# Transpose instructions for turned operands, grouped gathering of modulation units, and two modulation loads asked for later in a two-block transformer kernel

## What is computed

```
for l in (0, 1):                                   # first block, 2 layers of 3 sublayers
    mod = silu(c) @ ada_w[l] + ada_b[l]            # shift, scale, gate for each sublayer, for context and latent
    h = rms_norm(x) * g * (1 + scale) + shift      # before every sublayer
    x = x + 0.5 * gate * swiglu(h)                 # sublayers k = 0, 2, 3, 5
    x = x + gate * gated_delta(h)                  # sublayer k = 1 (two directions, chunks, 8 heads of 128)
    x = x + gate * window_attention(h)             # sublayer k = 4
for l in (0, 1):                                   # second block, latent tokens only
    x = layer_norm(a * x + mixer(x)); x = layer_norm(a * x + conv_ffn(x))
# gated_delta, per chunk: gc = cumsum(g); decay = exp(gc[i] - gc[j]) for i >= j;
# a triangular solve with (beta k k^T) * decay, a state carried between chunks, rms_norm per head
```

## Time and profile before

| | |
|---|---|
| median of 3 runs | 3239.9 us (3236.26 to 3246.45) |
| the profiled execution | 3243.84 us, its span 3241.9 us |
| TensorE busy | 3051.2 us, 94% |
| ScalarE, VectorE, GpSimd busy | 35%, 41%, 48% |
| mean granted TensorE clock | 0.968 of 2.4 GHz |
| DMA | 389.91 MB, mean 120 GB/s |

### The profile page before, as it was taken

The page is one execution under the profiler, slowest core; times in us unless marked ns, Lnnn a source line. Parts: engine busy times, 40 slices in busy tenths (PEclk is TensorE's granted clock), DMA queues, the critical chain, the costliest instruction groups (busy, mean ns, idle before and its releaser), DMA issues.

```text
span 3241.9 us, 54462 instructions
## 1 busy us (share of the span) xinstructions
PE 3051.2 (94%) x22484; PEld 2659.8 (82%) x22484; DVE 1341.2 (41%) x2506; ACT 1149.5 (35%) x1769; POOL 1564.1 (48%) x1207
## 2 busy tenths in 40 slices
PE   5999999999998999998999979889999999999998
PEld 4787778889887787776778876889987998987998
DVE  3222246755554321233212356333455551445551
ACT  2212223323422322213222235333444664444563
POOL 1444444322123344443445530687853688654686
PEclk8999999999998999998999989999999999999999
DMA  7434332210002334434332320344441444441443
GB/s 288 168 124 169 121 108 91 86 45 3 2 3 78 130 123 169 151 115 155 119 135 87 115 80 14 117 176 154 178 156 66 142 169 169 147 153 66 143 171 127
DMA packets 58915, 389.91 MB, mean 120 GB/s; under 512 B 6480, under 2 KB 7760, under 8 KB 21360
## 3 DMA queue, kind: packets, MB, share of 16 engines
q1 hardware_dynamic: 49472, 322.07, 27.7%
q10 hardware_dynamic: 9072, 64.12, 5.5%
q0 software_dynamic: 192, 1.18, 0.1%
HBM read 386.29 MB, written 1.05 MB: 119 GB/s over the span
## 4 chain that ended last, share of the span: by engine, by line
PE 62%; POOL 18%; issue 13%; DVE 3%; ACT 2%; DMA 0%; POOLq 0%; ACTq 0%; DVEq 0%
POOL ring_lo L2619 18%; PE bank L647 16%; PE bank L648 15%; PE bank L649 15%; PE bank L682 2%; PE bank L1244 1%; PE bank L1149 1%; PE bank L1255 1%; PE bank L971 1%; PE bank L936 1%; PE bank L709 1%; PE bank L1137 1%; PE bank L828 1%; DVE core L2519 0%; PE bank L983 0%
## 5 line engine op out<-in xcount | busy, mean ns | idle before, releaser
L2619 POOL TENSOR_TENSOR ring_lo<-ring,w_hi 128x512 fp32r<-128x512 f32 (+1 forms) x832 | 1094.8, 1347 | 1246.5 <-ACT w_hi L1401 1246.1
L649 PE MATMUL bank<-h_hi,ring_lo 128*128 128x256 f32 (+1 forms) x3384 | 1117.6, 330 | 0.0
L647 PE MATMUL bank<-h_hi,w_hi 128*128 128x512 f32 (+1 forms) x2448 | 863.5, 353 | 51.7 <-POOL ring_lo L2619 28.6
L648 PE MATMUL bank<-h_lo,w_hi 128*128 128x512 f32 (+1 forms) x2448 | 849.1, 347 | 0.0
L649 PEld LDWEIGHTS bank<-h_hi,ring_lo 128*128 128x128 f32 x3384 | 652.5, 193 | 59.5 <-issue 0.5
L647 PEld LDWEIGHTS bank<-h_hi,w_hi 128*128 128x128 f32 x2448 | 469.4, 192 | 131.0 <-issue 50.1
L1401 ACT ACTIVATE w_hi<-ring 128x2048 fp32r<-128x2048 f32 (+2 forms) x226 | 395.2, 1749 | 413.3 <-PE bank L649 328.3
L648 PEld LDWEIGHTS bank<-h_lo,w_hi 128*128 128x128 f32 x2448 | 469.9, 192 | 52.8
L649 PE MATMUL bank<-hid_r,ring_lo 128*128 128x256 f32 (+1 forms) x1088 | 364.3, 335 | 0.0
L2025 DVE SCALAR_TENSOR_TENSOR core<-core,bank 128x512 f32<-128x512 f32 (+1 forms) x88 | 54.7, 621 | 651.8 <-ACT core L1469 651.8
L647 PE MATMUL bank<-hid_r,w_hi 128*128 128x512 f32 (+1 forms) x808 | 289.9, 359 | 2.3 <-POOL ring_lo L2619 2.3
(11 more groups left out here) (413 smaller groups left out, 4471.2 us busy)
## 6 DMA issues: line engine op xcount, KB each, us to landing
ring<-w SPq DMA_DIRECT2D x88, 1024.0 KB, 4.8
zbuf<-ada_later ACTq DMA_DIRECT2D x60, 1024.0 KB, 4.8
ring<-up SPq DMA_DIRECT2D x48, 1024.0 KB, 4.8
ring<-w SPq DMA_DIRECT2D x64, 704.0 KB, 4.0
ring<-mla_in SPq DMA_DIRECT2D x24, 1024.0 KB, 4.8
ring<-down SPq DMA_DIRECT2D x32, 768.0 KB, 4.3
ring<-dn_in SPq DMA_DIRECT2D x16, 1024.0 KB, 4.8
ring<-ada SPq DMA_DIRECT2D x12, 1024.0 KB, 12.3
```

Of the source, the lines that this page charges most:

```text
L647: pe.matmul(out, a[0], b[0], start=start, stop=False)
L648: pe.matmul(out, a[0], b[1], start=False, stop=False)
L649: return pe.matmul(out, a[1], b[0], start=False, stop=stop)
L2619: ins = pool.tensor_tensor(like(ring_lo[:, r, a:b], part), like(ring[:, r, a:b], part), part.bitcast(F32), ALU.subtract)
```

## The change

It has five parts. (1) Where a matmul against the identity served as a transpose (`spread`, `value_turn`, `key_turn`, the head spreads of `delta_out`, `layer_norm`), the transpose instruction of TensorE stands now. (2) `decay_row` is such a transpose as well, of the cumulated column `TOK_GC`, where it was a matmul of `TOK_G` with the triangle. (3) Units of the modulation inside the feed-forward halves are gathered: `cond` is six columns wider and its two filled columns stand at 6 and 7, so that a slice that begins at 6 - 2r puts unit r's results into rows 2r and 2r+1 of each strip and adds zeros to the others; four units of `w1` (two of `w2`) accumulate in the same bank, and one copy by ScalarE and two matmuls (output 128 x 4 x 2) sum all of them. (4) `sel` has 8 columns instead of 2. (5) The first two loads of `ada_later` for sublayer 1 are issued by ScalarE after `norm(0)` and `pair_take` instead of ahead of them.

```diff
-CONSTS = [("eps", 1), ("sel", 2), ...
+GROUPS = 4
+CONSTS = [("eps", 1), ("sel", 8), ...
-        if r % 32 < 2:
+        if r % 32 < 8:
-        cond = sb("cond", [P, DC, 32])
+        cond = sb("cond", [P, DC, 38])
...
 def spread(k, t0):
-    mm = pe.matmul(psum[STAT][:, tc * P:(tc + 1) * P], norm_r[:, tc:tc + 1].broadcast_to([P, P]), ident, start=True, stop=True)
+    mm = pe.transpose(psum[STAT][:, tc * P:(tc + 1) * P], norm_r[:, tc:tc + 1].broadcast_to([P, P]), ident)
...
-def partials(out, w):
+def partials(out, w, row=0, first=True, last=True):
     for c in range(DC):
         j = c % 4
-        mm = pe.matmul(out[32 * j:32 * j + 32, :], cond[:, c, :], w[...], start=(c < 4), stop=(c >= 4))
+        mm = pe.matmul(out[32 * j:32 * j + 32, :], cond[:, c, 6 - 2 * row:38 - 2 * row], w[...],
+                       start=(first and c < 4), stop=(last and c >= 4))
...
-def ada_sum(m, g, b):
-    pe.wait_ge(ada_out, ada_count(m, g) + 1)
+def ada_sum(m, group, g, rows):
+    pe.wait_ge(ada_out, group + (GROUPS * m + 1))
     for q in range(2):
-        mm = pe.matmul(psum[MISC][:, bass.ds(g * 4 + 2 * q, 2)], ada_ev[:, b, q * 128:(q + 1) * 128], sel, ...)
+        at = psum[MISC][:, bass.ds(g * 4, 4 * rows)].rearrange("p (v f) -> p v f", f=4)
+        mm = pe.matmul(at[:, :, 2 * q:2 * q + 2], ada_ev[:, q * 128:(q + 1) * 128], sel[:, 0:2 * rows], ...)
...
-ada_part(m, i * 2 + u // 2, u % 2)
+ada_part(m, i * 2 + u // 2, u % 2, u, u == 0, u == 3)
-if m is not None and not isinstance(n, int):
-    ada_sum(m, n, u % 2)
+if m is not None and not isinstance(n, int) and u == 3:
+    ada_sum(m, i, i * 4, 4)
...
-if m is not None and u % 2 == 0:
-    ada_sum(m, i * 2 + (8 + u // 2), u // 2)
+if m is not None and u == 2:
+    ada_sum(m, i + 2, i * 2 + 8, 2)
...
 def decay_row(U, s):
-    mm = pe.matmul(dbank[s][A0][:, hd, :], dcol(TOK_G, U, s, hd).broadcast_to([P, P]), incl(s), start=True, stop=True)
+    mm = pe.transpose(dbank[s][A0][:, hd, :], dcol(TOK_GC, U, s, hd).broadcast_to([P, P]), ident)
...
 def value_turn(U, s):
-    mm = pe.matmul(dbank[s][A1][:, hd, :], feat(2, U, s, hd), ident, start=True, stop=True)
+    mm = pe.transpose(dbank[s][A1][:, hd, :], feat(2, U, s, hd), ident)
...
 # key_turn, delta_out and layer_norm in the same way
...
 # ScalarE
 def norm(k, t0):
-    if (k, 0) in MOD_IN:
+    if k > 0 and (k, 0) in MOD_IN:
         for g in range(2):
             load_ada(MOD_IN[k, 0], g, g)
...
 def slot(n, i, u, hf=hf):
     if m is not None and not isinstance(n, int):
-        ada_take(m, n, u % 2)
+        if u == 3:
+            ada_take(m, n)
         load_ada(m, n + 2, u % 2)
...
     for p in range(HEAD_UNITS // 2, UNITS // 2):
         pair_take(p)
+    for g in range(2):
+        load_ada(0, g, g)
     first_highs("w1_000")
...
 # VectorE
-dve.tensor_scalar(cond[:, :, 0:2], ctmp[:, :, :], 0.5, None, ALU.mult).then_inc(cond_done, 1)
+dve.tensor_scalar(cond[:, :, 6:8], ctmp[:, :, :], 0.5, None, ALU.mult).then_inc(cond_done, 1)
-dve.wait_ge(ada_summed, UNITS * (m + 1))
+dve.wait_ge(ada_summed, GROUPS * (m + 1))
```

More of the change, by code:

```diff
@@ L117 @@
 PW = dict(PARAMS)
-CONSTS = [("eps", 1), ("sel", 2), ("ident", 128), ("ones", 128), ("identc", 64), ("level", 2 * LEVELS * 64), ("incl", 2 * 128)]
-NFIRST = 1 + 2 + 128 + 128
+CONSTS = [("eps", 1), ("sel", 8), ("ident", 128), ("ones", 128), ("identc", 64), ("level", 2 * LEVELS * 64), ("incl", 2 * 128)]
+NFIRST = 1 + 8 + 128 + 128
 COFF = {}
@@ L280, in build @@
         ada_pair = core[:, 4096:6144].rearrange("p (b f) -> p b f", b=4)
-        ada_ev = core[:, 4096:4608].rearrange("p (b f) -> p b f", b=2)
+        ada_ev = core[:, 4096:4352]
         ada_w = zbuf[:, 0:2 * SLOT].rearrange("p (b f) -> p b f", b=2)
@@ L673, in spread @@
                 for tc in range(t0 // P, T // P):
-                    mm = pe.matmul(psum[STAT][:, tc * P:(tc + 1) * P], norm_r[:, tc:tc + 1].broadcast_to([P, P]), ident,
-                                   start=True, stop=True)
+                    mm = pe.transpose(psum[STAT][:, tc * P:(tc + 1) * P], norm_r[:, tc:tc + 1].broadcast_to([P, P]), ident)
                 mm.then_inc(spread_done, 1)
-            def partials(out, w):
+            def partials(out, w, row=0, first=True, last=True):
                 for c in range(DC):
                     j = c % 4
-                    mm = pe.matmul(out[32 * j:32 * j + 32, :], cond[:, c, :], w[:, c * 256:(c + 1) * 256],
-                                   start=(c < 4), stop=(c >= 4))
+                    mm = pe.matmul(out[32 * j:32 * j + 32, :], cond[:, c, 6 - 2 * row:38 - 2 * row], w[:, c * 256:(c + 1) * 256],
+                                   start=(first and c < 4), stop=(last and c >= 4))
                 return mm
@@ L878, in key_turn @@
                         for hd in range(QUAD):
-                            mm = pe.matmul(dbank[s][A1][:, hd, :], feat(1, U, s, hd), ident, start=True, stop=True)
+                            mm = pe.transpose(dbank[s][A1][:, hd, :], feat(1, U, s, hd), ident)
                         mm.then_inc(dn["kt"][s], 1)
@@ L1054, in delta_out @@
                     for tc in range(4):
-                        mm = pe.matmul(psum[HEAD_BANKS[hd % 6]][:, tc * P:(tc + 1) * P],
-                                       head_r[:, tc * DNH + hd:tc * DNH + hd + 1].broadcast_to([P, P]), ident, start=True, stop=True)
+                        mm = pe.transpose(psum[HEAD_BANKS[hd % 6]][:, tc * P:(tc + 1) * P],
+                                          head_r[:, tc * DNH + hd:tc * DNH + hd + 1].broadcast_to([P, P]), ident)
                     mm.then_inc(hd_spread, 1)
@@ L1347, in layer_norm @@
                 for tc in range(2):
-                    mm = pe.matmul(psum[STAT][:, tc * P:(tc + 1) * P], ln_r[:, tc:tc + 1].broadcast_to([P, P]), ident, start=True, stop=True)
+                    mm = pe.transpose(psum[STAT][:, tc * P:(tc + 1) * P], ln_r[:, tc:tc + 1].broadcast_to([P, P]), ident)
                 mm.then_inc(ln_pe, 1)
```

19 lines of the change are left out of this document (10 added, 9 removed).

## The result

**3183.2 us** (median of 5 executions) against 3239.7 us (median of 5) for the kernel before: ratio 0.9821, interval 0.9803 to 0.9838, which is 52 to 64 us less. 3191 us was predicted, with a range of 3177 to 3218. In two more sessions the changed kernel gave medians of 3189.7 and 3185.8 us, ratios 0.9856 (0.9819 to 0.9893) and 0.9817 (0.9792 to 0.9843).

What follows compares the result with a forecast made beforehand. TensorE was taken to bound the feed-forward halves and delta core, transfers the start. Terms 18.0 + 16 + 5.7 + 3.8 + 5.2 = 48.7 us, off 3239.9, gave 3191 us; range 3177 to 3218.

Steps and rivals of the forecast that it cites:

- The gathered units: Feed-forward halves: 40 of 60 modulation sums leave TensorE's stream at 0.45 us each, 18.0 us less.
- 8 as free: Gathered sums: the matmul's 8 output columns instead of 2 cost nothing, at worst under 1 us.
- The core: Delta core: 18 blocks of transposes save 0.99 us each, 17.8 us, less one clock fall of 1.8: 16 us.
- rival (c): Delta core: the turns were cover, ScalarE or VectorE waits replace them; gain 5 instead of 16, 3202 us; chance 0.12.
- Rival (a): Transposes cost two passes or the like, parts 1 and 2 give nothing: 22.7 us gain, 3217 us; chance 0.12.
- Rival (b): Transposes cost a quarter: nine us more in the core, 60 us gain in all, 3180 us; chance 0.18.
- Rival (d): Delta core: transposes don't hold the clock, which falls to 1.2 GHz: 84 us more, 3275 us; chance 0.04.
- the 1.8 us: Delta core: deduction for one more clock fall, a `new_values` block taking 3.78 us at 1.2 GHz against 1.98.
- The head spreads: `delta_out`: halved records let the second slot begin 3.8 us sooner, limited by GpSimd's subtractions ending at 1005.9.
- halved, TensorE could begin the products 4.7 us earlier: Head spreads of `delta_out`: 64 records fill 9.7 us; halving them frees TensorE 4.7 us sooner.
- The spreads and layer norms: Norms on bare chains: halved records save 3.8 us in spreads of k = 1 to 5, 1.9 in four layer norms.
- The start: Before `w1`: later loads let head units land sooner, 4.7 us, plus 0.5 for the k = 0 spread.

Runs made afterwards that it cites:

- the norms alone: Kernel before with only the transposes of `spread`, `layer_norm` and `delta_out`: 3230.2 us, ratio 0.9955.
- the loads alone: Kernel before with only the two `ada_later` loads issued later, after `pair_take`: 3237.7 us, ratio 0.9988.
- the edit on the kernel before: Kernel before with the hidden product kept in its PSUM bank and both instructions reading it there: 3233.9 us, ratio 0.9983.
- the sums alone: Kernel before with only the gathered modulation units (parts 3 and 4): 3218.8 us, ratio 0.9936.

## Why the prediction was right

**The gathered units** (18.0 us; measured 18.1 in the table, 20.6 alone). Count, price and "8 as free" all held.

**The core** (16 us; measured 15.6, and 18.3 alone). One record per transpose was taken, bound by its load, at 0.124 us. The one record held, and so did the price: 0.127 us in a block of eight, 0.109 for each one added. That the load is what bounds it is not shown. One unit of the changed kernel's timeline, the three turns and what answers beside them:

```profile
711.70 1.10 PE L880 MATMUL bank<-con,big 128*128 128x128 f32 x8
711.82 0.60 ACT L1828 ACTIVATE core<-bank 128x512 f32<-128x512 f32 x1 [0.34 <-PE bank L903]
...
712.73 0.68 PE L912 MATMUL bank<-core 64*64 64x64 f32 x16
...
714.74 1.09 PE L829 MATMUL bank<-con,tok 128*128 128x128 f32 x8
...
715.20 0.41 DVE L2518 TENSOR_TENSOR core<-bank,near 128x256 f32<-128x256 f32 x1
...
715.76 0.68 PE L923 MATMUL bank<-core 64*64 64x64 f32 x16
```

From a turn's start to the next block is 1.03 and 1.02 us, where 0.99 was said and 1.98 stood before: a gain of 0.96 a block, 17.3 for 18. `fourths` starts at 712.73, after ScalarE's copy has ended at 712.42, and `diagonals` at 715.76, after VectorE's end at 715.61: the answers are still there first, now by 0.15 to 0.3 us. These waits of TensorE in the core confirm it:

```profile
PE bank L972 <- ACT core L1846: 7.0, 8, 1.3
PE bank L937 <- DVE core L2524: 4.2, 16, 0.3
...
PE bank L937 <- ACT core L1832: 1.2, 5, 0.2
```

They were 7.0, 4.3 and 1.2 us before. No wait took the turns' place, so rival (c) fell. Rival (a) fell with the record counts. Rival (b) fell with 0.109 to 0.127 us a transpose against 0.248 for the matmul. By the Trainium skill ("TensorE: Matmul & The Clock Gate", Terms), four times faster for FP32, a block would have been 0.5 us; the measured factor here is 1.9 to 2.3, and the measurement decides. Rival (d) fell with the granted clock of the core, 0.93 to 0.95 before, 0.95 after and 0.95 with the transposes doubled. Part 4 of the same page of the Trainium skill says that the full clock doesn't engage for transposes. The trace differs: in the head spreads (below) the clock rose from 0.50 while TensorE did transposes alone.

What failed inside the term is the place of the correction: the 1.8 us were taken off for one more fall at a unit's end (`new_values`). Five of its eight blocks are at the lower level before and after. The loss lies elsewhere. From one unit's first `decay_row` to the next unit's (for the last, to the first head spread), the gain is 0.9 to 1.0 us a block in five of the eight units. In the first it is 1.4 us for three blocks, in the second 3.1 for two, in the fourth -0.4 for one. The turns of the first unit did give 3.1 us (7.25 before, 4.11 after); but its `squares` met the lower level and took 3.3 us instead of 2.0. In the fourth unit the clock fell in the middle of `updates`. The first line is of the changed kernel and the second of the kernel before, at the same place (granted clock in the last column but two):

```profile
757.80:761.80 4.00, 4.00 (x82) 3.99 (x81) 1.24 (x3) 0.00 (x0) 0.60 (x1) 0.57 0.02 4
780.60:784.60 4.00, 3.75 (x93) 3.60 (x93) 1.82 (x5) 0.60 (x2) 1.63 (x2) 1.00 0.01 4
```

The sum of these is 1.7 us under 18 blocks of 0.96. The size was right and the place wrong, and with a core that moves by some 3 us without an edit, that the size came out so well is partly luck.

**The head spreads** (3.8 us; measured 3.1). The failed step is "halved, TensorE could begin the products 4.7 us earlier". These windows hold the granted clock, the last column but two, of the changed kernel's head spreads:

```profile
956.90:961.50 4.60, 4.60 (x22) 4.60 (x23) 3.34 (x5) 1.59 (x3) 3.04 (x3) 0.50 0.00 0
961.50:963.20 1.70, 1.70 (x11) 1.70 (x10) 1.70 (x4) 0.93 (x2) 0.00 (x0) 0.60 0.00 0
```

and these are of the kernel before:

```profile
988.00:991.00 3.00, 3.00 (x14) 3.00 (x15) 0.75 (x1) 0.04 (x1) 3.00 (x3) 0.50 0.02 5
993.00:997.40 4.40, 4.40 (x42) 4.40 (x41) 4.28 (x8) 2.10 (x4) 0.00 (x0) 1.00 0.00 0
```

After a wait of 2.7 us TensorE runs at 1.2 GHz in both. Before, 42 of the 64 records were then done at 2.4 GHz, at 0.105 us each; the 32 transposes lie almost wholly in the stretch at 1.2 GHz, at 0.2 each. So the block went from 9.5 to 6.4 us, not to 4.7. From the first product to the second slot is 12.2 us in both traces: the second slot is bound by TensorE there, and GpSimd's low part, which I had named as late next, ends 0.5 us before it. That limit was right, though, and nearly reached. In the norms alone and with the core's transposes doubled the head spreads took 5.9 and 5.5 us, and there the second slot waited for that low part, 18.15 us after the first head spread in both; that is 3.6 less than before, where 3.8 was said. TensorE's wait at the second slot, in the norms alone and in the changed kernel:

```profile
PE bank L647 <- POOL ring_lo L2618: 1.1, 1, 1.1
```

```profile
PE bank L648 <- DVE x L2014: 1.1, 1, 1.1
```

**The spreads and layer norms** (5.7 us; measured 6.0). 0.96 us a spread instead of 0.89; that of k = 5 gave nothing instead of 0.3, which had been reckoned at the full clock. The window of that spread in the changed kernel, and in the kernel before:

```profile
2011.30:2012.10 0.80, 0.69 (x2) 0.29 (x2) 0.02 (x1) 0.00 (x0) 0.80 (x2) 0.50 0.42 174
```

```profile
2060.20:2061.00 0.80, 0.71 (x4) 0.52 (x4) 0.01 (x1) 0.00 (x0) 0.80 (x2) 1.00 0.35 143
```

Two records took 0.69 us at a granted clock of 0.50, where the four of before took 0.71 at 1.00.

**The start** (5.2 us; measured 6.3, 4.5 by the loads alone). The mechanism held, and the size is as uncertain as the transfers: the start of the kernel before varied by 2.7 us between its three profiles.

**The whole.** 49.1 us in the change's own steps against 48.7 predicted; the median fell by 56.5. The rest is, as far as it could be shown, a stall of the kernel before, 8.8 us of TensorE's waiting for VectorE, which the prediction did not look at, as it was in no part of the change. It was absent in both profiles of the changed kernel at its usual time; but 2 of its 13 executions, at 3196.2 and 3200.5 us, lie some 8 us and more above all the others, and may have had it. By the edit on the kernel before it is worth some 5 us on average, which with 49 makes 54, inside the measured 52 to 64. What stays open is why the changed kernel meets it less often, if it does: the sums alone and the loads alone have no long cast and the norms alone has one, by one profile each. Where the cast falls within a subtraction doesn't decide it, as it began 0.17 to 0.18 us after the start of one in the five profiles with the stall, and 0.16 to 0.18 in the five without. It was not tried to shift that place alone by a fraction of a microsecond.

## What to carry to other kernels

Read the price of a block from its start to the next block's, and ask at which clock level it will run: here the work behind a wait of 2.7 us began at 1.2 GHz, and halving it took away the fast end, not the slow beginning. Going from 2 to 8 output columns in a small matmul cost nothing here, so sums that are made one by one can be gathered behind one weight load. And look in the profile of before for single instructions that are ten times longer than their group: a stall that comes in some executions is otherwise counted for or against the change.

## What the hardware showed that I had not expected

VectorE was held for 11.8 to 12.4 us by a run of GpSimd instructions without a gap, not for the length of one of them. The Trainium skill ("SBUF — State Buffer", Who interferes with whom) says that the two engines share a port pair, that the one which issues first holds it for the whole instruction, and that a VectorE instruction with two SBUF inputs, or a cast in a two-port mode, contends for it with GpSimd. The trace agrees as to which instructions are held (the cast, and the subtraction with two SBUF inputs; neither with an input in PSUM); but by that rule the wait should end with the current subtraction, as it does in the changed kernel (1.28 us for the whole cast, GpSimd's subtractions there being 1.3 to 1.5 us long), and here it lasted for ten of them. Why GpSimd's next instructions went first is not shown. It also works the other way; GpSimd's largest group, first in the changed kernel, then in the changed kernel with the product in PSUM:

```profile
L2624 POOL TENSOR_TENSOR ring_lo<-ring,w_hi 128x512 fp32r<-128x512 f32 (+1 forms) x832 | 1094.9, 1346 | 1201.1 <-ACT w_hi L1402 1200.8
```

```profile
L2624 POOL TENSOR_TENSOR ring_lo<-ring,w_hi 128x512 fp32r<-128x512 f32 (+1 forms) x832 | 1062.1, 1308 | 1232.5 <-ACT w_hi L1402 1232.2
```

GpSimd is busy for 33 us less by an edit on VectorE (32 us less on the kernel before, too: 1094.8 to 1063.1). The doubled transposes showed one more such hold at another place, 13.95 us for a subtraction of two SBUF inputs in a layer norm (2637.26 us), in a kernel in which the first was absent.
